# First norm of a two-layer diffusion backbone: statistics beside the loads, conditioning in two groups

## The reference

```python
def modulation(cond, w_mod, b_mod):
    m = jax.nn.silu(cond) @ w_mod + b_mod          # (1, 6 * 1024)
    return jnp.split(m, 6, axis=-1)

def modulate(x, g, shift, scale):                   # x (tokens, 1024)
    y = x * lax.rsqrt(jnp.mean(x * x, axis=-1, keepdims=True) + EPS) * g
    return y * (1.0 + scale[:, None, :]) + shift[:, None, :]

sh1, sc1, gt1, sh2, sc2, gt2 = modulation(c, w_mod[l], b_mod[l])            # latent tokens
csh1, csc1, cgt1, csh2, csc2, cgt2 = modulation(c_ctx[None, :], w_mod[l], b_mod[l])
pl = modulate(xl, g_mix[l], sh1, sc1) @ w_in[l]
pc = modulate(xc, g_mix[l], csh1, csc1) @ w_in[l]
```

## Time and profile before

| what | value |
|---|---|
| median of three runs | 2357.04 us |
| the profiled execution | 2357.41 us |
| its span, first to last instruction | 2355.6 us |
| TensorE busy | 2082.0 us, 88% |
| VectorE, ScalarE, GpSimd busy | 1181.4, 749.4, 635.1 us |
| mean granted TensorE clock | 0.952 of full speed |
| start of the first statistics on VectorE | 41.3 us |
| start of the first feature matmul | 70.3 us |
| start of the attention's bias tables on TensorE | 90.2 us |

### The profile page before, as it was taken

The page is one execution under the profiler, slowest core; times in us unless marked ns, Lnnn a source line. Parts: engine busy times, 40 slices in busy tenths (PEclk is TensorE's granted clock), DMA queues, the critical chain, the costliest instruction groups (busy, mean ns, idle before and its releaser), DMA issues.

```text
span 2355.6 us, 29264 instructions
## 1 busy us (share of the span) xinstructions
PE 2082.0 (88%) x11392; PEld 1710.9 (73%) x11392; DVE 1181.4 (50%) x2112; ACT 749.4 (32%) x1208; POOL 635.1 (27%) x820
## 2 busy tenths in 40 slices
PE   1776899989989799999999967788989887999999
PEld 0565788866667588888888864677866665878887
DVE  1554643357885566346616555564457874211112
ACT  2232223255663311111111132332264653222222
POOL 0111021121011233333333412113131103555555
PEclk9888999999998799999999988999899998999999
DMA  7200143110000143323323311001011001332333
GB/s 271 75 27 19 38 161 108 37 36 27 10 19 26 37 143 108 99 99 108 118 80 108 108 47 36 19 29 54 28 45 36 19 9 46 97 98 90 98 97 100
DMA packets 76239, 165.53 MB, mean 70 GB/s; under 512 B 5192, under 2 KB 46664, under 8 KB 75088
## 3 DMA queue, kind: packets, MB, share of 16 engines
q1 hardware_dynamic: 75728, 163.28, 20.9%
q10 hardware_dynamic: 384, 0.47, 0.1%
HBM read 161.63 MB, written 2.10 MB: 70 GB/s over the span
## 4 chain that ended last, share of the span: by engine, by line
PE 76%; DVE 11%; ACT 5%; issue 4%; DMA 1%; POOL 1%; SPq 1%; PEld 0%; PEldq 0%; DVEq 0%; ACTq 0%; POOLq 0%
PE psum L1011 21%; PE psum L1013 21%; PE psum L1012 21%; DMA marope<-c_rope 1%; PE psum L1540 1%; DVE naptlo L1877 1%; PE psum L1062 1%; POOL wlo L499 1%; DVE n_t L1754 1%; PE psum L1093 1%; PE psum L1180 1%; DVE n_t L1782 1%; DVE hlo L1774 1%; PE psum L1309 1%; PE psum L1295 1%
## 5 line engine op out<-in xcount | busy, mean ns | idle before, releaser
L499 POOL TENSOR_TENSOR wlo<-raw,whi 128x256 fp32r<-128x256 f32 x816 | 634.9, 810 | 1712.6 <-ACT whi L525 1712.6
L1011 PE MATMUL psum<-hhi,whi 128*128 128x512 f32 (+1 forms) x1640 | 592.2, 361 | 36.1 <-DVE hlo L1774 14.6
L1012 PE MATMUL psum<-hlo,whi 128*128 128x512 f32 (+1 forms) x1640 | 583.6, 356 | 0.0
L1013 PE MATMUL psum<-hhi,wlo 128*128 128x512 f32 (+1 forms) x1640 | 583.5, 356 | 0.0
L525 ACT ACTIVATE whi<-raw 128x1024 fp32r<-128x1024 f32 x204 | 215.4, 1059 | 943.1 <-PE psum L1013 942.4
L1011 PEld LDWEIGHTS psum<-hhi,whi 128*128 128x128 f32 x1640 | 316.3, 193 | 92.6 <-issue 22.9
L1013 PEld LDWEIGHTS psum<-hhi,wlo 128*128 128x128 f32 x1640 | 315.6, 192 | 43.4
L1012 PEld LDWEIGHTS psum<-hlo,whi 128*128 128x128 f32 x1640 | 316.6, 193 | 40.3
L2306 DVE TENSOR_TENSOR ffuf<-ffsa,psum 128x768 f32<-128x768 f32 (+1 forms) x44 | 36.1, 821 | 348.8 <-ACT ffsa L968 348.8
L2291 DVE SCALAR_TENSOR_TENSOR ffmacc<-wm,csil,ffmacc 128x256 f32<-128x256 f32 x336 | 189.7, 605 | 10.1 <-DVE ffmacc L2291 4.9
L1011 PE MATMUL psum<-uhi,whi 128*128 128x512 f32 (+1 forms) x528 | 189.0, 358 | 2.6 <-DVE ulo L2310 1.5
(11 more groups left out here) (305 smaller groups left out, 3408.2 us busy)
## 6 DMA issues: line engine op xcount, KB each, us to landing
raw<-w_stream SPq DMA_DIRECT2D x204, 512.0 KB, 3.6
wm<-w_mod SPq DMA_DIRECT2D x80, 512.0 KB, 3.9
wm<-w_mod SPq DMA_DIRECT2D x8, 1024.0 KB, 18.3
xres<-x_t SPq DMA_DIRECT2D x8, 384.0 KB, 6.6
out<-xres SPq DMA_DIRECT2D x8, 256.0 KB, 2.4
consts<-c_f SPq DMA_DIRECT2D x1, 353.0 KB, 7.8
narpb<-rpb ACTq DMA_DIRECT2D x2, 120.0 KB
mlmask<-c_gate ACTq DMA_DIRECT2D x2, 108.0 KB
```

Source lines behind the costliest of these rows:

```text
L499: ins = nc.gpsimd.tensor_tensor(wlo[:, q % 2, c:c + UW // 4], raw[:, q % RAW, c:c + UW // 4], whi[:, q % 2, c:c + UW // 4], ALU.subtract)
L1011: mm(dst, ah, bh, start=first, stop=False)
L1012: mm(dst, ah, bl, start=False, stop=False)
L1013: return mm(dst, al, bh, start=False, stop=last)
```

## The change

Five things are edited. The wait for the rope table moves from the head of VectorE's list to behind the first norm. The four blocks of conditioning weights are loaded in the order 0, 2, 1, 3, and the first two `raw` units stand behind the first and the second block. The eight chunks are made in the order 0, 1, 4, 5, 2, 3, 6, 7: the first four give shift and scale of tiles 0 to 3, the last four those of tiles 4 to 7. VectorE takes each group by itself (`head_take`, new). On TensorE the first group stands ahead of tile 0, two chunks of the second group between tiles 0 and 1, and the last two between tiles 1 and 2. On ScalarE the matching row copies stand between the `hhi` of tiles 1 and 2 and of tiles 3 and 4. The turned columns land in bank 7, and the last four chunks share bank 6, where they had four banks. The load of the small table `rpb` is issued earlier.

```diff
@@ constants
+HEAD_ORDER = (0, 1, 4, 5, 2, 3, 6, 7)
@@ sync
-            for c in range(MOD_HEAD // 2):
+            for n in range(0, MOD_HEAD, 2):
+                c = HEAD_ORDER[n] // 2
                 for half in range(2):
                     sp.dma_start(NRM["wm0"][:, c, 4 * half:4 * half + 4, :],
                                  w_mod[0, c, :, 4 * half:4 * half + 4, :]).then_inc(mod0_in[c], 16)
-                if c == 0:
-                    loads(0, 2)
+                if n < 4:
+                    load(n // 2)
@@ scalar, norm_phase
                 if l == 0 and which == 0:
-                    for n in range(MOD_HEAD):
-                        mod_row_of(0, n, bank(n % 4)[:, 0:256])
-                        if n == 3:
-                            his(2)
+                    head_rows(0, 1)
+                    his(1)
+                    head_rows(2, 3)
+                    his(2)
+                    small(NA["rb"][:, :], rpb[0])
                 for k in range(KT):
+                    if l == 0 and which == 0 and k in (2, 4):
+                        head_rows(k + 2, k + 3)
                     act.wait_ge(t_done, n0 + k + 1)
@@ tensor
-            def mod_head():
-
-                pe.wait_ge(csil_zero, 1)
-                pe.wait_ge(act_chain, 1)
-                for n in range(MOD_HEAD):
-                    pe.wait_ge(mod0_in[n // 2], 32)
-                    if n >= 4:
-                        pe.wait_ge(mod_row, n - 3)
-                    mod_chunk(0, n, bank(n % 4), lambda half: NRM["wm0"][:, n // 2, 4 * half:4 * half + 4, 256 * (n % 2):256 * (n % 2) + 256])
-                    if n >= 2:
-                        mod_turn(0, n - 2, bank(4))
-                mod_turn(0, MOD_HEAD - 2, bank(4))
-                mod_turn(0, MOD_HEAD - 1, bank(4))
+            def mod_head(first, past):
+
+                for at in range(first, past):
+                    n = HEAD_ORDER[at]
+                    c = n // 2
+                    pe.wait_ge(mod0_in[c], 32)
+                    if at >= 4:
+                        pe.wait_ge(mod_row, at)
+                    mod_chunk(0, n, bank(at if at < 4 else 6),
+                              lambda half: NRM["wm0"][:, c, 4 * half:4 * half + 4, 256 * (n % 2):256 * (n % 2) + 256])
+                    if at == 4:
+                        pe.wait_ge(mod_add, 1)
+                    if at > first:
+                        mod_turn(0, HEAD_ORDER[at - 1], bank(7), at - 1)
+                mod_turn(0, HEAD_ORDER[past - 1], bank(7), past - 1)
@@ tensor, na_inputs
-                (ah, al), (bh, bl) = unit(ua), unit(ub)
                 for k in range(KT):
+                    if l == 0 and k < 3:
+                        mod_head(*((0, 4), (4, 6), (6, 8))[k])
+                    if k % 4 == 0:
+                        wh, wl = unit((ua, ub)[k // 4])
                     pe.wait_ge(h_lo, 16 * l + k + 1)
@@ vector
+            def head_take(k0, k1):
+
+                dve.wait_ge(mod_tr, k1)
...
+                mod_mix(0, 0, k0, k1)
@@ vector, norm_phase
-                if l == 0 and which == 0:
-                    mod_take(0, 0, MOD_HEAD, bank(4))
-                    mod_mix(0, 0)
                 dve.wait_ge(r_done, 2 * l + which + 1)
...
                 for k in range(KT):
+                    fresh = l == 0 and which == 0 and k in (0, 4)
+                    if fresh and k:
+                        lower(k - 1)
+                    if fresh:
+                        head_take(k, k + 4)
...
-                    if k:
+                    if k and not fresh:
                         lower(k - 1)
@@ vector, head of the list
             dve.wait_ge(const_in, 48)
-            dve.wait_ge(rope_in, 16)
...
                 norm_phase(l, 0, True)
                 seq(V.drain())
+                if l == 0:
+                    dve.wait_ge(rope_in, 16)
                 na_inputs(l)
```

More of the change, by code:

```diff
@@ L578, in norm_phase, with head_rows @@
                 rsqrt_of(NRM["r"][:, q0:], psum_pair(psum, 3)[:, q0:], 1.0 / D_MODEL).then_inc(r_done, 1)
+                def head_rows(*at):
+                    for n in at:
+                        mod_row_of(0, n, bank(n if n < 4 else 6)[:, 0:256])
                 if l == 0 and which == 0:
-                    for n in range(MOD_HEAD):
-                        mod_row_of(0, n, bank(n % 4)[:, 0:256])
-                        if n == 3:
-                            his(2)
+                    head_rows(0, 1)
[3 more added lines that the diff above has]
+                    small(NA["rb"][:, :], rpb[0])
                 for k in range(KT):
+                    if l == 0 and which == 0 and k in (2, 4):
+                        head_rows(k + 2, k + 3)
                     act.wait_ge(t_done, n0 + k + 1)
@@ L593, in na_inputs @@
             def na_inputs(l):
-                small(NA["rb"][:, :], rpb[l])
+                if l:
+                    small(NA["rb"][:, :], rpb[l])
                 act.wait_ge(w_used, u0(l, NA_V) + 2)
@@ L1064, in mod_chunk, with mod_turn @@
                     ins.then_inc(mod_c, 1)
-            def mod_turn(l, n, dst):
-                e = l * MODC + n
+            def mod_turn(l, n, dst, e=None):
+                e = l * MODC + n if e is None else e
                 pe.wait_ge(mod_row, e + 1)
@@ L1113, in norm_phase @@
                     pe.wait_ge(const_in, 48)
+                    pe.wait_ge(csil_zero, 1)
+                    pe.wait_ge(act_chain, 1)
                 pe.wait_ge(sq_used, 8 * (2 * l + which) + KT)
@@ L1121, in na_inputs @@
                 ua, ub = u0(l, NA_V), u0(l, NA_V) + 1
-                (ah, al), (bh, bl) = unit(ua), unit(ub)
                 for k in range(KT):
+                    if l == 0 and k < 3:
+                        mod_head(*((0, 4), (4, 6), (6, 8))[k])
+                    if k % 4 == 0:
+                        wh, wl = unit((ua, ub)[k // 4])
                     pe.wait_ge(h_lo, 16 * l + k + 1)
-                    wh, wl = (ah, al) if k < 4 else (bh, bl)
                     c = 256 * (k % 4)
@@ L1396, in ml_pe @@
                         if l == 0:
-                            pe.wait_ge(mod_add, 3)
+                            pe.wait_ge(mod_add, 4)
                         turn_out(0, "x", bank(5))
@@ L1685, in _ @@
                 norm_phase(l, 0, True)
-                if l == 0:
-                    mod_head()
                 na_inputs(l)
@@ L1738, in mod_take, with mod_mix @@
                 dve.wait_ge(mod_add, taken[0])
-            def mod_mix(l, w):
+            def mod_mix(l, w, k0=0, k1=KT):
                 for c in range(2):
-                    ins = V.scalar_tensor_tensor(amix[:, l, w, :, c], mods[:, l, 24 * w + 8:24 * w + 16, c], 1.0,
-                                                 lc[:, l, C_GMIX + 8 * w:C_GMIX + 8 * w + 8], ALU.add, ALU.mult)
+                    ins = V.scalar_tensor_tensor(amix[:, l, w, k0:k1, c], mods[:, l, 24 * w + 8 + k0:24 * w + 8 + k1, c], 1.0,
+                                                 lc[:, l, C_GMIX + 8 * w + k0:C_GMIX + 8 * w + k1], ALU.add, ALU.mult)
                 seq(ins)
+            def head_take(k0, k1):
+                dve.wait_ge(mod_tr, k1)
+                pick = lambda x: x.rearrange("p (w k c) -> p w k c", w=2, c=2)[:, :, k0:k1, :]
+                bias = lc[:, 0, C_BMOD:C_BMOD + 2 * KT].rearrange("p (w k) -> p w k", w=2)[:, :, k0:k1]
+                V.tensor_tensor(mods[:, 0, 0:2 * KT, :].rearrange("p (w k) c -> p w k c", w=2)[:, :, k0:k1, :],
+                                pick(bank(7)[:, 0:4 * KT]), bias.unsqueeze(3).broadcast_to([P, 2, k1 - k0, 2]), ALU.add)\
+                    .then_inc(mod_add, 1)
+                taken[0] += 1
+                dve.wait_ge(mod_add, taken[0])
+                mod_mix(0, 0, k0, k1)
             def add_square(l, which, full, k):
```

## The result

Three runs of the changed kernel gave 2327.32, 2328.15 and 2331.25 us, median 2328.15 against 2357.04 before: ratio 0.988, 95% interval 0.9858 to 0.9903, 28.9 us. A second series of six runs gave 2333.18 against 2356.04 before (0.9897, 0.988 to 0.9915), 22.9 us, inside the range. The profiled execution of the first series took 2327.32 us with a span of 2325.5, 30.1 us less than before. Bias tables of the attention now start at 64.98 instead of 90.2 us, so 25.2 us of these come ahead of them and 4.9 us behind them.

What follows compares the result with a forecast made beforehand. The start was taken to be bound by VectorE's misplaced rope-table wait, the rest by TensorE's pace. Rope wait -26.2, first group -4.8, features +7.5 net -23.5 us, giving 2333.5 us from 2357.04, range 2329 to 2341.

Steps and rivals of the forecast that it cites:

- The rope wait: VectorE's start: without the wait for the rope table it starts 26.2 us earlier, so the statistics end at 26.1 us.
- The first group: TensorE's first four chunks and turns: from statistics at 26.1 to the last turn's end at 33.8 us, block 2 arriving in time.
- The new neighbour: GpSimd's subtractions for unit 1 beside VectorE's scalings of tiles 0 and 1: a loss of 1.3 us, features from 39.3.
- The features: TensorE's eight tiles with later chunks between: 27.3 us instead of 19.85, low clock over tile 0, VectorE pacing tiles 4 to 7.
- Bias tables: Stage right behind the features, whose last matmuls were forecast to end at 66.6 us instead of 90.1.
- The rest of the program: Everything behind the features keeps its distance to their end, with no change in length.
- one of my signs of being wrong: The forecast is wrong if stages behind 90 us change their length by more than 2 us.
- the lasting low clock: Rival: TensorE's clock stays low over tiles 1 to 3 and later chunks, 7.1 us more, time 2340.6; 13 in 100.
- the case without both costs: Rival: no loss beside GpSimd and no clock fall in TensorE's pause, gain 27.2 us, time 2329.8; 9 in 100.
- the one in which the split costs more than it brings: Rival: early statistics do not come, slowed amid the loads, and the split costs up to +2.7 us, 2359.7; 2 in 100.

Runs made afterwards that it cites:

- rope_only: Kernel before with only the rope-table wait moved behind the first norm; bias tables at 68.51 us, median 2337.05 us against 2356.04 before (0.9913).
- split_only: Changed kernel with the rope-table wait put back at the head of VectorE's list; bias tables at 92.67 us, median 2359.61 against 2356.04 before (1.0015).
- again: Changed kernel profiled a second time, no edit; bias tables at 66.08 us, 2278.4 us behind them, median of that series 2333.18 us.
- third: Changed kernel profiled a third time, no edit; bias tables at 65.67 us, 2266.3 us behind them.
- old_loads: Changed kernel with conditioning weight blocks loaded in the old order 0, 1, 2, 3; bias tables at 70.45 us, median 2336.06 against 2355.07 before (0.9919).
- no_neighbour: Changed kernel with weight unit 1's high part made after tile 1's instead of ahead of tile 0; bias tables at 62.92 us, median 2332.54 us (0.99 of before).
- best: Changed kernel with chunks 5 and 6 ahead of tile 0, last two behind it, unit 1's high part late, 5 extra matmuls; median 2331.58 us (0.9901 of before).
- filled: Changed kernel with 12 unused extra matmuls on TensorE ahead of tile 0; bias tables at 63.08 us, median 2327.61 against 2355.07 before (0.9878).
- rope_filled: Kernel before with the rope-table wait moved behind the norm, plus 6 unused matmuls ahead of the seventh chunk and 8 ahead of tile 0; median 2330.97 us (0.9908).
- both: Changed kernel with unit 1's high part after tile 1's and 8 unused matmuls ahead of tile 0; bias tables at 61.45 us, median 2329.05 against 2353.23 before (0.9908).

## Why the prediction was right

* **The rope wait.** Forecast -26.2 us at the statistics' end, measured -27.0 (25.34 against 52.33): the last table landed 0.7 us earlier than before. `rope_only` and `split_only` show that this step carries the gain: alone it moves the bias tables to 68.5, and without it the change is a loss.
* **The first group.** Forecast 7.7 us from the statistics' end to the end of the last turn, measured 6.4 (7.1 in `again`, 7.5 in `third`). For the first profile the term was mis-sized: I took two chunks at the low level (3.31 us), and in the first profile both took 1.96, nearly all at the high one; in `again` and `third` they took 3.01 and 3.33. The granted clock reads 1.00 there in all of them, as it does ahead of the first recorded change also while TensorE works, so the level is read from the chunks' length. No wait for block 2, as forecast: its second half was issued at 9.07 and took 15.9 us to land, 25.0, and its first chunk started at 28.08, a margin of 3.1 us. In the old order (`old_loads`) the block came at 32.45.
* **The new neighbour.** Forecast 1.3 us, measured 1.37 in the scalings (3.57 against 2.20) and another 0.56 in the mix, which I had left out (0.80 against 0.24). `no_neighbour` shows both to be GpSimd's. The rule of the Trainium skill (SBUF - State Buffer, section "Who interferes with whom") that two such instructions contend holds in kind: both engines were slowed, GpSimd's four from 2.80 to 3.40 us. In size it was 0.34 us for each of the four scalings, not the 0.95 that I had drawn from a strict reading.
* **The features.** Forecast 27.3 us, measured 27.34, 27.86 and 26.59: a low clock over tile 0 and no longer, the row copies 0.6 us each, tiles 2 and 3 hidden behind the second group. TensorE did tile 1 from 45.91, 8.27 us behind its first feature matmul; forecast 8.3. The end was right by another path than forecast. I had VectorE's pace set it, 2.24 us a tile up to tile 7; VectorE had no further scaling ahead of tile 7's rest, finished it at 61.69, and TensorE came to that tile at 62.6. So TensorE's own matmuls, six tiles in 13.2 us from 51.79, bounded the end. The forecast had them beside VectorE's chain with 0.2 us between the two, so the sum did not suffer; that is luck of a near tie.
* **Bias tables** at 66.6 in the forecast, 65.0, 66.1 and 65.7 in the profiles: a gain of 23.5 forecast, 24.2 between the means.
* **The rest of the program.** "All keeps its distance" is true of the program and wrong by some microseconds for one execution. The first profile was 4.9 us shorter there; the repeats were longer by 0.9 and 13.0 us than the first profile before. A change of more than 2 us there was one of my signs of being wrong, and by that sign the forecast fails in two of the three profiles; but the kernel before differs by 3.7 us from itself in the same part. That the first median came out just below the range, and the second where the forecast was, is scatter and no merit or fault of the sum.

Of the rivals, the lasting low clock did not come in any profile of the changed kernel, the case without both costs neither; the one in which the split costs more than it brings was right in its price (2.7 us forecast, 2.4 at the bias tables in `split_only`) and wrong only in that the statistics did come early: amid loads at 419 GB/s the seven adds took 0.97 us each, as before.

## What to carry to other kernels

Look at which transfer the first instruction of an idle engine waits for, and whether the work behind it reads it: one wait in the wrong place in an in-order list cost 21 us here, and everything else in this change 3. Work that is cut in two to start earlier pays in row copies and in pauses between the pieces; by itself it lost 2.4 us or more, beside the moved wait it brought 3, and with the clock kept up only 0.5. Where a change is worth a few microseconds and the clock scatters the whole time by more, compare the time of the landmark right behind the edit, in several profiles, and not the medians.

## What the hardware showed

* In `rope_only`, `old_loads` and `best` a pause of TensorE of about 3 us among chunks and turns went with a fall of the granted clock to 0.50: within the pause, 1.3 us behind its end, and at its end. A chunk then took 1.9 us for 1.07. Pauses are not the whole cause: in the kernel before it fell at 65.8, with the turns still running. Matmuls without a use in such a pause kept it at 1.00 (`filled`, `rope_filled`, `both`) and gave back 1.3 to 4.9 us. In `filled` itself it fell again at 66 to 68 us, in the bias stage, where the longest of TensorE's waits for VectorE is 2.5 us.
* Over whole executions of one program the span went from 2325.5 to 2344.5 us with the mean granted clock from 0.954 to 0.945.
* GpSimd beside VectorE lengthened even VectorE's tiny instructions on 128x4 floats, from 0.24 to 0.80 us for the two.
